# Three, two, two and none of every eight expert rows are added to x by VectorE instead of TensorE

## The reference, cut to what matters

```
u_e = jnp.take(u_tab, expert, axis=0)
v_e = jnp.take(v_tab, expert, axis=0)
act = jax.nn.gelu(jnp.einsum('chkd,cd->chk', u_e, xc))
return jnp.einsum('chk,chkd->cd', gate * act, v_e)      # added to x
```

## Time and profile before

| | us |
|---|---|
| median of 3 runs (1857.91 to 1860.49) | 1858.96 |
| the profiled execution | 1857.8 |
| its span, from the first to the last instruction | 1855.8 |
| TensorE busy | 1653.5 (89%) |
| VectorE busy | 1163.6 (63%) |
| ScalarE busy | 618.9 (33%) |
| the 2048 expert MATMULs of L661 | 971.5 |
| the 512 dots of L1425 | 625.8 |
| bytes over all DMA queues | 687.19 MB, mean 370 GB/s |

### The profile page before, as it was taken

How to read it: one execution, slowest core, us unless ns; L and a number is a source line. 1 busy time by engine, 2 the same in 40 slices (tenths; PEclk the granted TensorE clock), 3 DMA queues, 4 the chain that set the end, 5 groups by cost and what they waited for, 6 DMA issues and landing times.

```text
span 1855.8 us, 19751 instructions
## 1 busy us (share of the span) xinstructions
PE 1653.5 (89%) x6720; PEld 998.4 (54%) x6720; DVE 1163.6 (63%) x3290; ACT 618.9 (33%) x1477; POOL 563.5 (30%) x525
## 2 busy tenths in 40 slices
PE   5898889999799999999998988999999987777776
PEld 5786666644446666765564644654554632322222
DVE  5521157985696435697756556897666567766764
ACT  3122232254344223226533223237343132222221
POOL 0000023333243212333333333333433344443431
PEclk8999999999899999999999999999999999999999
DMA  5425599999899889999999999999999999999996
GB/s 208 168 97 177 203 391 421 420 345 410 319 421 422 362 316 400 390 420 355 422 421 422 421 421 421 421 385 357 418 420 421 421 421 422 421 421 421 420 420 250
DMA packets 95827, 687.19 MB, mean 370 GB/s; under 512 B 10608, under 2 KB 10864, under 8 KB 13040
## 3 DMA queue, kind: packets, MB, share of 16 engines
q0 software_dynamic: 73728, 536.90, 70.8%
q1 hardware_dynamic: 22000, 149.04, 20.3%
HBM read 684.85 MB, written 1.05 MB: 370 GB/s over the span
## 4 chain that ended last, share of the span: by engine, by line
PE 61%; DMA 25%; DVE 7%; ACT 4%; issue 2%; POOL 1%; DVEq 0%; ACTq 0%; SPq 0%; POOLq 0%
PE bank L661 30%; DMA slots<-expert_rows,expert 23%; PE bank L309 12%; PE bank L475 5%; PE bank L651 3%; DVE slots L1425 3%; PE bank L648 3%; DMA ring<-w_blocks 2%; PE bank L376 1%; PE bank L346 1%; PE bank L363 1%; PE bank L420 1%; ACT diag L1031 1%; PE bank L562 1%; PE bank L422 1%
## 5 line engine op out<-in xcount | busy, mean ns | idle before, releaser
L661 PE MATMUL bank<-slots,diag 128*128 128x512 f32 x2048 | 971.5, 610 | 147.2 <-ACT diag L1031 143.6
L752 POOL DMA_INDIRECT slots<-expert_rows,expert x512 | 561.9, 1098 | 1264.8 <-PE bank L661 1007.1
L1425 DVE CUSTOM_DVE_ANT_0 slots<-slots,htok 128x1024 f32<-128x1024 f32 x512 | 625.8, 1222 | 337.1 <-DMA slots<-expert_rows,expert 335.9
L661 PEld LDWEIGHTS bank<-slots,diag 128*128 128x128 f32 x2048 | 374.2, 193 | 582.6 <-issue 344.0
L309 PEld LDWEIGHTS bank<-hT,ring 128*128 128x128 f32 x2432 | 295.5, 194 | 65.5 <-issue 64.2
L309 PE MATMUL bank<-hT,ring 128*128 128x128 f32 x2432 | 297.8, 278 | 8.5 <-DMA ring<-w_blocks 4.7
L1051 ACT ACTIVATE gel<-dot 128x2 f32<-128x2 f32 x256 | 52.0, 203 | 655.4 <-DVE dot L1425 654.8
L1031 ACT ACTIVATE diag<-ident,coef 128x128 f32<-128x128 f32 x512 | 178.7, 394 | 154.2 <-DVE coef L1059 141.8
L1059 DVE SCALAR_TENSOR_TENSOR coef<-gel,ginv,gexp 128x2 f32<-128x2 f32 x256 | 54.1, 211 | 133.0 <-ACT gel L1051 131.3
L1051 ACT ACT_TABLE_LOAD x66 | 84.7, 1283 | 1.2
L1059 DVE SCALAR_TENSOR_TENSOR sg<-pad,prm,sg 128x128 f32<-128x128 f32 x240 | 70.3, 342 | 0.0
(11 more groups left out here) (242 smaller groups left out, 1363.1 us busy)
## 6 DMA issues: line engine op xcount, KB each, us to landing
ring<-w_blocks SPq DMA_DIRECT2D x132, 1024.0 KB, 9.1
slots<-expert_rows,expert POOLq DMA_INDIRECT x512, 13.4
products<-gain_rows SPq DMA_DIRECT2D x5, 512.0 KB, 12.3
keys<-w_blocks SPq DMA_DIRECT2D x2, 1024.0 KB, 11.1
prm<-small SPq DMA_DIRECT2D x2, 768.0 KB, 10.9
x<-x_rows SPq DMA_DIRECT2D x2, 512.0 KB, 4.7
slots<-mem_rows SPq DMA_DIRECT2D x1, 1024.0 KB, 12.0
products<-mem_rows SPq DMA_DIRECT2D x1, 1024.0 KB, 11.9
```

The lines of the kernel that those rows point to most:

```text
L661: last = mm(bank[i][:, :], diag[:, n % DIAGS, :], slots[:, n % SLOTS, D + i * 512:D + (i + 1) * 512], start=m == 0, stop=m == PER - 1)
L752: nc.gpsimd.indirect_dma_start(slots[:, n % SLOTS, :], None, experts_d, bass.IndirectOffsetOnAxis(ap=idx[q % 2][:, k:k + 1], axis=0),).the ...
L1425: v.tensor_tensor_reduce(out=slots[:, s, 0:D], in0=slots[:, s, 0:D], in1=htok[:, ph % 2, :], scale=1.0, scalar=0.0, op0=ALU.mult, op1=ALU.add,
```

## The change

A table names which of every eight experts VectorE adds: numbers 2, 4 and 7 in stage 0, 2 and 6 in stages 1 and 2, none in stage 3. That is 48 + 32 + 32 = 112 of 512. For such an expert ScalarE writes no diagonal and TensorE issues nothing. VectorE issues one SCALAR_TENSOR_TENSOR over 128x1024 that reads the v half of the slot, the coefficient and x, and writes x; its end releases the slot (`slot_added`), and it waits for the add before it. All adds stand in ticks with an even expert number: that of expert 2, 4 or 6 directly behind the dot two ticks later, that of expert 7 at the end of the next tick. Waits that counted all experts now count those of one engine (`TAKEN`).

```
+BY_VECTOR = [(2, 4, 7), (2, 6), (2, 6), ()]
+TAKER = ["vector" if n % SLOTS in BY_VECTOR[n // PER] else "tensor" for n in range(NG)]
+TAKEN = [TAKER[:n].count(TAKER[n]) for n in range(NG)]
...
-                if 0 <= tick - G0 - 2 < NG:
-                    add_expert(tick - G0 - 2)
+                n = tick - G0 - 2
+                if 0 <= n < NG and TAKER[n] == "tensor":
+                    add_expert(n)
...
-                    eng.wait_ge(slot_used, n - SLOTS + 1)
+                    before = n - SLOTS
+                    eng.wait_ge(slot_used if TAKER[before] == "tensor" else slot_added, TAKEN[before] + 1)
...
-                    diagonal(n - 2)
-                    diagonal(n - 1)
+                    for k in (n - 2, n - 1):
+                        if TAKER[k] == "tensor":
+                            diagonal(k)
...
+            def add_slot(n):
+
+                q, k = divmod(n, TOP)
+                xs = x[:, n // PER % NC, :]
+                eng.wait_ge(coef_ready, n // 2 + 1)
+                if TAKEN[n]:
+                    eng.wait_ge(slot_added, TAKEN[n])
+                stt(xs, slots[:, n % SLOTS, D:2 * D], coef[:, q % 2, k:k + 1], xs, ALU.mult, ALU.add)\
+                    .then_inc(slot_added, 1)
...
             def add_to_x(ph):
-                eng.wait_ge(slot_used, PER * (ph + 1))
+                eng.wait_ge(slot_used, TAKER[:PER * (ph + 1)].count("tensor"))
+                eng.wait_ge(slot_added, TAKER[:PER * (ph + 1)].count("vector"))
...
                     dot_of(n)
+                if 2 <= n <= NG + 1 and TAKER[n - 2] == "vector" and n % 2 == 0:
+                    add_slot(n - 2)
                 go_on(strands, tick)
                 go_on(route, tick)
+                if 2 <= n <= NG and n % 2 == 0 and TAKER[n - 1] == "vector":
+                    add_slot(n - 1)
```

More of the change, by code:

```diff
@@ L270, in build @@
         slot_used = sem("slot_used")
+        slot_added = sem("slot_added")
         x_added = sem("x_added")
@@ L656, in add_expert @@
                 ph, m = divmod(n, PER)
-                if m == 0 and ph:
+                mine = [k for k in range(PER * ph, PER * (ph + 1)) if TAKER[k] == "tensor"]
+                if n == mine[0] and ph:
                     eng.wait_ge(x_added, 2 * ph)
[L659 to L663, removed]
+                i = TAKEN[n]
+                eng.wait_ge(diag_ready, i + 1)
+                for h in range(2):
+                    last = mm(bank[h][:, :], diag[:, i % DIAGS, :],
+                              slots[:, n % SLOTS, D + h * 512:D + (h + 1) * 512],
+                              start=n == mine[0], stop=n == mine[-1])
                 last.then_inc(slot_used, 1)
@@ L1028, in diagonal @@
                 q, k = divmod(n, TOP)
-                if n >= DIAGS:
-                    eng.wait_ge(slot_used, n - DIAGS + 1)
-                act(diag[:, n % DIAGS, :], ident[:, :], ACT.Copy, scale=coef[:, q % 2, k:k + 1])\
+                i = TAKEN[n]
+                if i >= DIAGS:
+                    eng.wait_ge(slot_used, i - DIAGS + 1)
+                act(diag[:, i % DIAGS, :], ident[:, :], ACT.Copy, scale=coef[:, q % 2, k:k + 1])\
                     .then_inc(diag_ready, 1)
```

## The result

The changed kernel takes 1872.38 us (median of 6 runs, 1864.07 to 1878.33) against 1859.43 (median of 6, 1857.91 to 1860.49). The ratio is 1.0062, interval 1.0036 to 1.0088: slower by 0.6%, where 1.5% faster was forecast. The profiled execution took 1872.86 us with a span of 1871.0.

A forecast was written before the change was run, and what follows sets the result against it. TensorE was taken as the bound only where DMA ran below its 421 GB/s ceiling. Relief of 36 us less 9 us for adds gives 27: the profiled 1857.8 becomes 1830.8, plus 1.2 for the median, 1832 us; range 1808 to 1858.

The forecast's parts named there:

- The ceiling: Stage 3, only experts, is bound by DMA at 421 GB/s; time can be won only where the rate is lower.
- The relief, 36 us: Time won by taking experts from TensorE in six stretches below the DMA ceiling: 8, 3, 10, 4, 5 and 6 us.
- The keys: Stretches at 640 to 720 and 720 to 780 us, where removing experts from TensorE was to win 10 and 4 us.
- The output products and attention at 380, 840 and 1240 us: Stretches with TensorE nearly always busy, where removing its experts was to win 8, 5 and 6 us.
- The adds, 9 us: Cost of 112 adds of 1.2 us on VectorE, felt only in its full stretches at 320, 520, 780 and 1160 us.
- the low end: Cost of the adds in VectorE's four full stretches if every idle moment of VectorE can be filled: 8.3 us.
- (c): Rival: VectorE's in-order dots set the pace wherever it was busy over 70%; adds cost 47 us against 36: 1870; chance 0.14.
- (b): Rival: where TensorE is relieved, weight ring or attention's handovers set the pace; 18 us of 36 left, less 9: 1850; chance 0.16.
- (a): Rival: waiting rows wholly absorb VectorE's overload and TensorE's relief comes through in full, 44.7 us: 1814; chance 0.22.
- (d): Rival: adds hold up GpSimd's gathers for their whole length and the DMA queue runs dry, 134 us: about 1957; chance 0.02.
- (c)'s sign: In the stretches of scans and taps, under 410 GB/s where it was 421, with VectorE at 100%.
- (b)'s sign: TensorE's waits for weight blocks grow by more than 10 us in total.

The follow-up runs named there:

- Experiment 2: Changed kernel with each of VectorE's 112 adds cut to the first of 1024 columns, TensorE relieved as in the change: 1854.64 us, ratio 0.9972.
- experiment 5: The change only for experts 88 to 143, where TensorE computes memory keys and values (19 adds), all others as in the kernel before: 1848.22 us, ratio 0.9939.
- experiment 10: Relief alone (adds cut to one of 1024 columns) for experts 16 to 63 of stages 0 to 2, otherwise the kernel before: 1862.13 us, ratio 1.0022.
- 11: As experiment 10, with two MATMULs of identity times zeros on TensorE in place of each removed expert's four: 1858.62 us, ratio 1.0005.
- Experiment 1: Changed kernel with four MATMULs of identity times zeros on TensorE for each removed expert but the last of stage 0: 1876.64 us, ratio 1.0101.
- 8: As experiment 7, with four MATMULs of identity times zeros on TensorE in place of each removed expert: 1871.41 us, ratio 1.0068.
- experiment 7: The change for experts 16 to 63 of stages 0 to 2 alone, other experts as in the kernel before: 1875.47 us, ratio 1.0082.
- 12: As experiment 5, with 2, 4, 6 and 7 of eight for experts 88 to 143, 28 adds in place of 19: 1846.37 us, ratio 0.9938.
- experiment 4: The change in stages 1 and 2 alone (2 and 6 of eight), stages 0 and 3 as in the kernel before: 1865.54 us, ratio 1.0040.
- experiment 3: The change in stage 0 alone (2, 4, 7 of eight), stages 1 to 3 as in the kernel before: 1857.30 us, ratio 0.9989.

## Why the prediction was wrong, point by point

**The ceiling** was right: no stretch of 20 us in any run moves more than 426 GB/s, and stage 3 is nearly as it was, 322.3 us from its first dot to its last against 320.5.

**The relief, 36 us, is the step that failed.** Experiment 2 measures 5. The keys had 10 + 4 = 14 of it, and measured 11 with the 19 adds in it (experiment 5): right within a few us, ring waits included. The output products and attention at 380, 840 and 1240 us had 8 + 5 + 6 = 19 us, and measured a loss of 4 (experiment 10). The working multiplied the experts in a stretch by 1.72 us because TensorE was busy for 97% of it. It took the handovers for the 1.2 to 1.5 us of idle that the rows showed. In the traces they were several times longer, 4.8 us for one (experiment 10), and hidden under the very experts that went away. A busy engine whose work is a mix of a dependent strand and of filler is not the bound of the strand.

**The clock** was not in the sum at all, though the earlier trace rows show what it does after a wait. Behind the wait of 4.7 us the next products took 3.62 us instead of 1.94, at 379 us. Experiments 10 and 11 give a first price for it inside, 3.5 us between them, although the faster one has more work on TensorE. That the clock alone makes this difference isn't shown; no run changed it by itself.

**The adds, 9 us,** were under-priced. Experiment 1 measures 17, within the bounds of 8.3 to 26.2 that the text gave. Unit and number were right (1280 ns, of which some 1.2 us until the next instruction; 112). What failed is the choice near the low end, on the ground that rows waiting in slots absorb the lag. By the dots at the borders of the four full stretches (320, 520, 780 and 1160 us) the lag grew by 5.0, 3.6, 3.1 and 6.3 us in experiment 1, where the low end has 3.7, 2.4, 2.2 and nothing; in the changed kernel it grew by 5.0, 3.5, 3.1 and 0.6. The waiting rows keep the DMA fed, but the strand's other engines wait for VectorE's late products at once, as TensorE did at 379 us. Each add stands ahead of the strands' pieces of its tick, all but that of expert 7; whether it would cost less behind them was not tried.

**The rivals.** (c) named 1870 us and the measured time is 1872, but it got there with adds at 47 us and relief at 36; both were too large, so the number is luck. Its mechanism, VectorE's in-order dots and strands as the pace, is the one that holds inside the stages, as far as experiments 1 and 8 show it. (b), handovers and ring take the gain back, is the one that holds for the relief; it left 18 us of the 36, and 5 are there. The two together make the result, and the prediction had given each a chance apart, with a sum for each apart. (a) is out.

(d), the gathers held up by the adds. The Trainium skill's rule about the shared port (SBUF — State Buffer, section "SBUF: two separate sides") agrees with the timeline of the changed kernel: the 152 gathers that start while VectorE is idle take 0.94 us each on the mean, the 174 that start during a dot 1.45, and the 24 that start during an add 1.46. But their mean over all rose from 1098 to 1153 ns only, 28 us over 512 gathers, and GpSimd idles for 1251 us beside them. The mean doesn't follow the number of adds either: with 42 adds (experiment 7) it is 1093 ns, and experiments 5 and 12, with 1109 and 1108 ns, are faster than before. No cost in time was found.

**The signs.** 448 MATMULs fewer, 112 adds and a stage 3 of the same length came true. The stretches of attention and output products didn't come near 421 GB/s but fell to 301, 305 and 312. Of (c)'s sign the first half came true: VectorE is busy for 59.0 of 60 us at 320, 38.8 of 40 at 520, 59.2 of 60 at 780 and 73.7 of 80 at 1160 us. The rate went under 410 GB/s only at 320 us (409), and was 416 to 421 at the others; what was missing came behind these stretches. (b)'s sign failed: TensorE waits for weight blocks 15.9 us in the changed kernel, against 11.7. Nor does the prediction's 9 us for stages 1 and 2 follow from its own terms, which give 4 + 5 + 6 - 2 = 13; measured were a loss of 6 (experiment 4) and, for stage 0, a gain of 2 instead of 15 (experiment 3).

**The range** had its upper end at 1858, where half of the relief meets a cost of 18; these two cancel, and the sum is 1859. It should have asked what happens if the relief is nothing. With the prediction's own upper bound of the cost that is 1859 + 26 = 1885, which would have covered the result.

## What to carry to other kernels

When filler is interleaved with a strand that hands over between engines, count the filler out before calling the engine the bound: lay the strand's own chain end to end, the other engines' parts and table loads with it, and only what is longer than this chain can be won. Move work off a busy engine where what stays on it is long independent work, here the products of keys and values; 19 moved experts won 11 us where all 112 lost 13. And an engine at 91 to 94% in a stretch had no room for more here, even with a buffer between it and the DMA.

## What the runs showed of the hardware

A kernel can get shorter by useless work on TensorE: with whole relief inside it had a granted clock of 0.84 in 60 us (1240 to 1300) and with two MATMULs of zeros for each removed expert 0.97, and the kernel was 3.5 us shorter. In the changed kernel a single wait of 4.7 us was followed by about 12 us at the half level (L384 at 379.27 to L671 at 387.49, each at twice its usual time). Products of identity with zeros, 444 among 6716 MATMULs, held the clock nearly as the real ones do (0.968 against 0.974 before). A gather takes 0.94 us on GpSimd when it starts beside an idle VectorE, and 1.45 us when it starts during a dot or an add over 128x1024.
